# One block of attention, recurrence and experts in float32: where the recurrence's output is finished in VectorE's order

## The reference, cut to what matters

```
def rwkv7_branch(p, w0, w2, a0, a2, g2, k_k, k_a, r_k, ln_g, ln_b):
    ...
    decay = jnp.exp(-jnp.exp(log_w))
    a = jax.nn.sigmoid(a0 + ad @ a2)
    g = jax.nn.sigmoid(gd) @ g2
    ...
    y = rwkv7_scan(rh, heads(decay), kh, vh, -kk, kk * ah)
    mu = jnp.mean(y, axis=-1, keepdims=True)
    var = jnp.mean(jnp.square(y - mu), axis=-1, keepdims=True)
    yn = ((y - mu) * lax.rsqrt(var + LN_X_EPS)).reshape(b, s, RWKV_WIDTH) * ln_g + ln_b
    bonus = jnp.sum((rh * kh * r_k).astype(jnp.float32), axis=-1, keepdims=True) * vh.astype(jnp.float32)
    out = (yn + bonus.reshape(b, s, RWKV_WIDTH)) * g
```

## Time and profile before

| what | us |
|---|---|
| median of 3 runs | 1864.32 (1860.89 to 1874.27) |
| profiled execution, its time | 1882.86 |
| its span | 1881.1 |
| TensorE busy | 1713.6 (91%) |
| VectorE busy | 1223.1 (65%) |
| ScalarE busy | 906.9 (48%) |
| GpSimd busy | 436.9 (23%) |

### The profile page before, as it was taken

One profiled execution on the slowest core, in us unless ns is written; L12 is line 12 of the kernel. 1 busy time (PEld: TensorE's weight loads), 2 busy tenths in 40 slices (PEclk: granted clock), 3 DMA queues, 4 the chain that ended last, 5 costly groups with the idle time before them and its releaser, 6 DMA issues. The chain is left out here.

```text
span 1881.1 us, 31801 instructions
## 1 busy us (share of the span) xinstructions
PE 1713.6 (91%) x12190; PEld 1404.0 (75%) x12190; DVE 1223.1 (65%) x1567; ACT 906.9 (48%) x1315; POOL 436.9 (23%) x633
## 2 busy tenths in 40 slices
PE   5999999999989977989899999268999999999976
PEld 5688888887878846878788788157888888888862
DVE  4655455430037745877453564658999999999966
ACT  1641111122137734545321322067888888888851
POOL 0100011200020015666420011012324334334312
PEclk9999999999989967978779999579999999999987
DMA  9368656431446411231534132637999999999966
GB/s 326 121 206 300 227 201 225 164 115 45 113 121 145 119 57 40 67 75 21 188 114 166 49 123 101 281 118 296 379 385 392 387 383 387 379 378 390 380 245 251
DMA packets 150799, 397.96 MB, mean 212 GB/s; under 512 B 51297, under 2 KB 67712, under 8 KB 129184
## 3 DMA queue, kind: packets, MB, share of 16 engines
q1 hardware_dynamic: 119200, 328.77, 48.4%
q0 software_dynamic: 16736, 41.34, 6.1%
q10 hardware_dynamic: 14752, 26.29, 3.7%
HBM read 342.79 MB, written 70.33 MB: 220 GB/s over the span
## 5 line engine op out<-in xcount | busy, mean ns | idle before, releaser
L2743 DVE TENSOR_TENSOR ex_w_r<-w,ex_w_r 128x1024 fp32r<-128x1024 f32 x384 | 451.7, 1219 | 25.0 <-ACT ex_w_r L2674 11.8
L2674 ACT ACTIVATE ex_w_r<-w 128x1024 fp32r<-128x1024 f32 x384 | 403.9, 1062 | 111.4 <-PE psum L2603 88.5
L2601 PE MATMUL psum<-ex_w_r,ex_x_t 128*128 128x512 f32 x512 | 204.4, 399 | 4.0 <-DVE ex_x_t L2743 2.4
L2603 PE MATMUL psum<-ex_w_r,ex_x_t 128*128 128x512 f32 x512 | 201.3, 393 | 0.0
L2602 PE MATMUL psum<-ex_w_r,ex_x_t 128*128 128x512 f32 x512 | 200.9, 392 | 0.0
L555 ACT ACTIVATE stage<-psum 128x512 f32<-128x512 f32 (+1 forms) x72 | 41.3, 574 | 299.7 <-PE psum L157 181.4
L155 PE MATMUL psum<-w_even,h_hi 128*128 128x512 f32 (+1 forms) x320 | 118.7, 371 | 4.4 <-ACT stage L555 4.4
L2554 POOL COPY ex_idx<-row_pair 128x1 int32 (+1 forms) x32 | 34.3, 1073 | 374.9 <-ACT ex_y L2674 374.9
L156 PE MATMUL psum<-w_even,h_hi 128*128 128x512 f32 (+1 forms) x320 | 118.4, 370 | 0.0
L157 PE MATMUL psum<-w_even,h_lo 128*128 128x512 f32 (+1 forms) x320 | 118.4, 370 | 0.0
L2601 PEld LDWEIGHTS psum<-ex_w_r,ex_x_t 128*128 128x128 f32 x512 | 97.1, 190 | 23.9 <-DVE ex_x_t L2743 2.8
(11 more groups left out here) (434 smaller groups left out, 3982.3 us busy)
## 6 DMA issues: line engine op xcount, KB each, us to landing
w<-in_exp_w SPq DMA_DIRECT2D x128, 1024.0 KB, 14.5
w<-in_exp_w SPq DMA_DIRECT2D x32, 2048.0 KB, 9.9
w_ring<-in_ada_w SPq DMA_DIRECT2D x12, 2048.0 KB, 11.2
w_ring<-in_w_in SPq DMA_DIRECT2D x10, 2048.0 KB, 10.6
qk<-stage_r ACTq DMA_DIRECT2D x16, 512.0 KB, 7.7
gates<-stage ACTq DMA_DIRECT2D x32, 256.0 KB, 2.0
bl_gates<-gates SPq DMA_DIRECT2D x8, 1024.0 KB, 4.8
w<-pair_rows SPq DMA_DIRECT2D x16, 512.0 KB, 9.7
```

What stands on the lines that cost most here:

```text
L2601: nc.tensor.matmul(out, lhs[0], hi, start=first, stop=False)
L2603: return nc.tensor.matmul(out, lhs[1], hi, start=False, stop=last)
L2674: return nc.scalar.activation(out, src, ACT.Copy)
L2743: return nc.vector.tensor_tensor(out, whole, high.bitcast(F32), ALU.subtract)
```

## The change

In the loop of the recurrence on VectorE, `y_finish` of tile `t - 2` stands behind `masked(1)` of tile `t + 1`; it stood ahead of `key_sums` of tile `t + 2`. Nothing else is changed.

```
                 at(t + 2, gate_half, unit_keys)
                 at(t + 1, masked(0))
-                at(t - 2, y_finish)
                 at(t + 2, key_sums)
                 at(t + 1, masked(1))
+                at(t - 2, y_finish)
                 at(t, bonus_values)
```

## The result

The kernel with the finish behind the second masked product takes 1875.49 us (median of 20 runs, 1869.51 to 1881.62). The kernel before takes 1865.20 us beside it (20 runs, 1860.89 to 1881.34). The ratio is 1.0055 with an interval of 1.0040 to 1.0069: 10.3 us more where 1.4 were forecast. The time lies inside the range, near its upper end.

The account below looks back on a forecast made before the run. TensorE, busy 91%, was taken as the bound, its order being the path in the affected part of the recurrence. Shifts of 0, -1.0, +0.7, +0.7 and +1.0 gave +1.4 us on 1864.32: 1865.7, range 1854 to 1877.

Parts of the forecast that it names:

- The second masked product comes earlier: VectorE in the recurrence: it starts at 772.79 in place of 775.64; the gate product's wait goes, at most 12.6 us.
- The gating's price: GpSimd's output gating after the finish: its duration, the one unknown price, with a low and a high estimate.
- the high end: Gating and VectorE's bonus work hold each other up: L1303 ends 3.54 us after the finish; sum +1.4 us.
- The low end: Gating on GpSimd takes 2.60 us, with 0.06 to start, as before the change; sum -3.2 us.
- rival 1: VectorE and GpSimd do not hold each other up: gating in 2.60 us, 1861.1 us; chance 0.20.
- `flip_lora`: TensorE's product waiting for the copy of the gates, with the next state behind it; its shift was counted per pass.
- A to D: First four of five affected recurrence passes; `flip_lora` shifts by 0.0, 1.0 earlier, 0.7 later and 0.7 later, in order.
- Pass E: the update: Fifth affected pass, without `flip_lora`: VectorE's state update 2.3 us later, 1.31 of it spare on TensorE, so 1.0 later.
- So I cost the clock at nothing: TensorE's hole in the passes only moves, ahead of `flip_lora`, 2.4 us as before; clock term zero.
- Rival 3: The new hole puts half clock over `advance(0)`, logits and offsets; first pass 4.7 us longer, 1870.4 us; chance 0.20.
- rival 2: The hole is split and TensorE's clock stays up in the passes: 10.6 us less, 1853.7 us; chance 0.10.
- The base: Whole kernel: median of three runs, 1864.32 us, taken as starting time instead of the profiled execution's 1882.86 us.

Follow-up runs that it names:

- run 4: The changed kernel with the finish still later, behind both bonus pieces (`bonus_values` and `bonuses`): 1883.39 us, ratio 1.0111.
- run 6: The changed kernel with three unread matrix products filling TensorE's hole between `keys_v` and `flip_lora`: 1858.64 us, ratio 0.9973 to the unchanged kernel.
- run 7: The unchanged kernel with two unread matrix products ahead of `gates`, where TensorE waits for the second masked product: 1856.58 us, ratio 0.9960.
- run 1: The changed kernel with a fourth gate buffer, so the copy of the gates no longer waits for the same pass's gating: 1870.94 us, ratio 1.0045.
- run 3: The unchanged kernel with only the key sums moved ahead of the finish, the second masked product staying behind it: 1854.64 us, ratio 0.9962.

## Why most steps of the prediction were right and its sum too small

*The second masked product comes earlier: right.* Forecast 772.79 for a pass that starts at 769.65, so 3.14 us behind the start; measured 774.21 - 771.10 = 3.11. L1869 takes 0.17 us and the wait of the gate product is gone.

*The gating's price: right.* The finish ends at 776.86 + 0.69 = 777.55, L1303 at 781.06: 3.51 us, forecast 3.54 by the high end. L1921 and L1922 take 1.64 and 1.63 us, as laid out. The low end and rival 1 fall. That the hold-up alone is not what costs the 10 us is shown from both sides: run 4 has the loss without it, run 6 has it (L1921 and L1922 at 1.6 us) without the loss.

*`flip_lora` right, the length of a pass not.* Counted from the pass's start, `flip_lora` is 0.1 us earlier in A, 1.1 earlier in B and 0.6 later in C and D (forecast 0.0, 1.0 earlier, 0.7 later). But a pass did not shift with its `flip_lora`: the lengths changed by +2.65, -1.94, -0.10 and -0.06 us. That these add up to 0.55, near the 0.4 of the forecast for A to D, is luck. With the clock up in both kernels the four passes differ by 1.5 us (runs 6 and 7).

*Pass E: the update right, what follows it too small.* The state's update comes at 904.28, 10.91 us behind the start, against 8.7 before: 2.2 later, forecast 2.3. The forecast took 1.31 us of TensorE's wait for the expansion off and put 1.0 us into the sum. It left out that TensorE then stands idle for 3.24 us, and that the product behind that hole runs at half clock (1.08 us where it took 0.61). The stretch from E's start to the last finish takes 73.3 and 73.6 us in after, against 71.5 in the second profile of before (73.8 in its first). With the holes filled nothing of this is left: 69.5 in run 6 against 69.6 in run 7, although the update in run 6 is as late as in after.

*The failed step: "So I cost the clock at nothing".* The hole is not "2.4 us as before". The two products ahead of it run at full clock and end 1.4 us earlier than I took for their half-clock length, so it is 3.78 us. The prediction says in its next sentence that this happens, and still puts a zero into the sum. The term measured 10.9 us for after over A to D (122.3 against 111.4 in run 6; 11.5 by its second profile). For before the same term is 6.7 us in its second profile (116.5 against 109.9 in run 7) and 11.9 in its first. So the change costs the clock about 4 us more, against an ordinary execution of before, and nothing against the one that I worked from. With 1.5 us for the longer passes and 1.8 to 2.1 from E on (73.3 and 73.6 us against 71.5) that makes about 8 of the 10.3 us measured; the part from E on belongs to the hole and the clock as well, as far as runs 6 and 7 show. The rest I can't place with two profiles of each kernel; what lies ahead of A varies by more.

The runs as a whole fit. Over the 89 executions of before listed beside the results, time falls with the mean granted clock, by 1.3 us for each 0.001 (correlation -0.93). Their mean clock is 0.9448, that of after (32 executions) 0.9408: by that slope some 5 us of the difference go with the clock. That is how times and clock go together, and no experiment of its own.

*Rival 3 is what happened.* Only because of it does the range reach as far as the measured time; the forecast itself was 10 us short. It had named the point: half clock at 781 to 790, over `advance(0)`, logits and offsets. The trace shows 0.52 from 781 to 788. Its price of 4.7 us was for one pass on top of a kernel that keeps its other losses. In fact all four passes take one and the same length, A growing by 2.65 us in the profiles that I compared and C by 4.0 against the second one. I gave this rival 0.20 and rival 2 (the clock stays up) 0.10. Rows 2 gave a reason to weigh it higher: each of passes A to D already had a stretch at half clock behind a hole of such a length, and the change was to put more of the path behind it.

*The base.* Taking the median of the runs and not the profiled execution was right. But the differences of the clock were read from one profile of an execution 18 us above it, where each of passes B to D is lost to the clock. That hid what there was to lose.

## What to carry to other kernels

Count what runs at half clock behind an idle hole of TensorE, and not only the hole's length. In pass A of before the half clock lay over 3.3 us with the gate product, and the pass was no longer than with the hole filled (27.77 against 28.60 us). In after it lay over the path to the next state, and the pass was 2.3 us longer than with the hole filled (30.42 against 28.15). Before taking work off one wait, follow whom the displaced work releases (here a buffer of gates, through GpSimd and ScalarE back to TensorE), and move the smallest piece first: the key sums alone gave 0.4% less, where moving the finish behind the masked product gave 0.55% more. Take a second profile when the profiled execution lies far from the median.

## What the runs showed of the hardware

- Products that nobody reads, put into TensorE's hole, made the kernel faster: 0.9973 of before in run 6 where after has 1.0055. The passes stayed at the 2.4 GHz level (granted 1.00) with a hole of 1.0 us, and fell to the 1.2 GHz level (0.52 over 781 to 788 us, 0.89 over each pass) in all eight passes of after's two profiles, with holes of up to 3.8 us.
- A short hole is no safeguard. In run 1 the clock fell behind 1.83 us, and behind 1.43 us it fell in one execution of before's pass C and not in the other. In pass A of run 3 it fell at 782 us with no idle piece longer than 0.65 us in the 20 us before. What decides whether it falls there is not shown.
- An operation of VectorE on 8 columns (L1869) takes 1.85 us when GpSimd's copy (L1324) and 128x512 addition (L1301) run beside it, and 0.17 us ahead of them. Larger ones take 1.63 instead of 0.69 us (L1922).
